# Down tiles from the 46th on turned by VectorE in squares of 32 by 32

## The reference

```python
h = modulate(rms_norm_2(x, norm_ffn[l]), sh2, sc2)        # (256, 1024)
q = (h @ w_query).reshape(B, S, PEER_HEADS, 2, HALF_KEY)   # 8 heads, two halves of 128
s1 = jnp.einsum('bshd,nd->bshn', q[..., 0, :], sub_keys1)
s2 = jnp.einsum('bshd,nd->bshn', q[..., 1, :], sub_keys2)
# top 16 of each, then the top 16 of their 256 sums: expert_idx, gates = softmax
u = jnp.take(expert_down, idx_blk, axis=0)                 # (16384, 1024) rows
act = jax.nn.gelu(jnp.einsum('bpd,bphkd->bphk', h_blk, u))
vv = jnp.take(expert_up, idx_blk, axis=0)
out = jnp.einsum('bphk,bphkd->bpd', g_blk * act, vv)
```

## Time and profile before

| | us |
|---|---|
| median of 3 runs | 1553.85 (1553.6 to 1555.4) |
| span of the profiled execution | 1550.4 |
| TensorE busy | 1510.6 (97%) |
| VectorE busy | 1013.9 (65%) |
| ScalarE busy | 663.4 (43%) |
| GpSimd busy | 425.8 (27%) |

### The profile page before, as it was taken

How to read it: one execution, slowest core, us unless ns; L and a number is a source line. 1 busy time by engine, 2 the same in 40 slices (tenths; PEclk the granted TensorE clock), 3 DMA queues, 4 the chain that set the end, 5 groups by cost and what they waited for, 6 DMA issues and landing times.

```text
span 1550.4 us, 25630 instructions
## 1 busy us (share of the span) xinstructions
PE 1510.6 (97%) x10099; PEld 1280.4 (83%) x10099; DVE 1013.9 (65%) x1829; ACT 663.4 (43%) x1009; POOL 425.8 (27%) x285
## 2 busy tenths in 40 slices
PE   8999999999999888999999999999999999999998
PEld 6777878875655575799999999999999888888887
DVE  5888787755765755678998733333334777777776
ACT  4455453633322511434434443434344444454553
POOL 0000000000011200018888888888882000000000
PEclk9999999999999999999999999999999999999999
DMA  9776664448655902446665656666663777777776
GB/s 342 268 261 226 209 239 137 162 163 258 227 207 175 407 19 67 160 147 178 137 150 137 148 139 148 140 144 143 146 142 95 239 239 242 240 238 238 239 239 231
DMA packets 166075, 297.25 MB, mean 192 GB/s; under 512 B 49539, under 2 KB 70323, under 8 KB 165957
## 3 DMA queue, kind: packets, MB, share of 16 engines
q1 hardware_dynamic: 119680, 277.08, 53.0%
q0 software_dynamic: 39296, 8.55, 7.6%
q10 hardware_dynamic: 6980, 9.99, 2.1%
HBM read 276.54 MB, written 19.03 MB: 191 GB/s over the span
## 4 chain that ended last, share of the span: by engine, by line
PE 91%; DVE 4%; issue 2%; ACT 1%; DMA 1%; SPq 0%; DVEq 0%
PE bank L553 23%; PE bank L555 22%; PE bank L557 22%; PE bank L1166 7%; PE bank L548 6%; PE bank L1097 1%; PE bank L1113 1%; PE bank L903 1%; PE bank L915 1%; PE bank L605 1%; PE bank L526 1%; PE bank L914 1%; DVE gt L1273 1%; PE bank L1157 0%; PE bank L598 0%
## 5 line engine op out<-in xcount | busy, mean ns | idle before, releaser
L2591 POOL DMA_INDIRECT c_dram<-gates,places x256 | 403.3, 1575 | 165.1 <-DVE gates L1962 87.5
L1292 DVE TENSOR_TENSOR dT_low<-bank,dT_high 128x512 fp32r<-128x512 f32 x256 | 165.0, 687 | 217.5 <-ACT dT_high L2488 150.6
L553 PE MATMUL bank<-hT_high,dT_high 128*128 128x256 f32 x1024 | 298.9, 292 | 0.1
L555 PE MATMUL bank<-hT_low,dT_high 128*128 128x256 f32 x1024 | 288.1, 281 | 0.0
L557 PE MATMUL bank<-hT_high,dT_low 128*128 128x256 f32 x1024 | 284.7, 278 | 0.0
L2500 ACT CAST up_high<-slot 128x1024 fp32r<-128x1024 f32 x128 | 134.5, 1051 | 160.1 <-DMA slot<-in_expert_up_dram 160.1
L553 PE MATMUL bank<-up_high,A_high 128*128 128x512 f32 x512 | 200.0, 391 | 1.2 <-DVE A_low L1292 1.2
L555 PE MATMUL bank<-up_low,A_high 128*128 128x512 f32 x512 | 200.7, 392 | 0.0
L557 PE MATMUL bank<-up_high,A_low 128*128 128x512 f32 x512 | 199.2, 389 | 0.0
L557 PEld LDWEIGHTS bank<-hT_high,dT_low 128*128 128x128 f32 x1024 | 193.4, 189 | 0.0
L553 PEld LDWEIGHTS bank<-hT_high,dT_high 128*128 128x128 f32 x1024 | 192.8, 188 | 0.3 <-issue 0.3
(11 more groups left out here) (449 smaller groups left out, 2370.5 us busy)
## 6 DMA issues: line engine op xcount, KB each, us to landing
slot<-in_expert_down_dram SPq DMA_DIRECT2D x128, 512.0 KB
slot<-in_expert_up_dram SPq DMA_DIRECT2D x128, 512.0 KB, 3.6
slot<-in_w_in_dram SPq DMA_DIRECT2D x41, 1024.0 KB, 5.4
P<-in_w_ada_dram SPq DMA_DIRECT2D x16, 1024.0 KB, 7.7
c_dram<-zeros SPq DMA_DIRECT2D x1, 16384.0 KB, 51.0
slot<-c_dram SPq DMA_DIRECT2D x128, 128.0 KB, 3.5
slot<-in_w_in_dram SPq DMA_DIRECT2D x6, 2048.0 KB, 8.4
slot<-in_w_out_dram SPq DMA_DIRECT2D x8, 1024.0 KB, 5.2
```

Source lines behind the costliest of these rows:

```text
L553: pe.matmul(o, lhsT=lhs_high.bitcast(F32R), rhs=rhs_high.bitcast(F32R), start=start, stop=False, skip_group_check=True)
L555: pe.matmul(o, lhsT=lhs_high.bitcast(F32R), rhs=rhs.bitcast(F32R), start=False, stop=False, skip_group_check=True)
L1292: return v.tensor_tensor(dst.bitcast(F32R), src, high, ALU.subtract)
L2591: g.indirect_dma_start(C_dram, bass.IndirectOffsetOnAxis(ap=places[:, x, k:k + 1], axis=0), gates[:, x, k:k + 1], None, compute_op=ALU.add ...
```

## The change

Tiles 0 to 44 are still turned by TensorE, tiles 45 to 127 (`BY_PE = 45`) by VectorE. The load of such a tile is split into four transfers, one for each group of 32 partitions; partition 32q+r gets, for m in 0..3, the 256 columns from 256q on of row 32m+r, in pieces of 1 KB. One `v.transpose` of 128x1024 turns all squares of 32 by 32 at once, reading every eighth column, and writes the whole turned tile, from SBUF to SBUF, into `dT_raw`, which lies where `dT_low` of that buffer lies. ScalarE copies it to `dT_high` in one instruction of 1024 columns, and VectorE subtracts in place. In VectorE's list, the turning of tile n+1 stands ahead of the subtraction of tile n and waits for the matmuls of tile n-2.

The squares give another order of inputs: block j holds the features 8p+j for partition p. So TensorE turns tiles 0 to 44 and the features `h3` from every eighth column too (`spread_block`), the query weights are loaded with rows 8p+j, and the rows 2, 3 and 5 of `modT` are loaded straight into that order (32 bytes per partition, three transfers), while only 24 rows of `mod_rows` are still turned.

```diff
--- before.py
+++ after.py
@@ -173,7 +173,7 @@
     state_ready, u_ready = sem("state_ready"), sem("u_ready")
     y_centred, y_squared, y_summed, y_rooted, bonus_v, y_done = (
         sem("y_centred"), sem("y_squared"), sem("y_summed"), sem("y_rooted"), sem("bonus_v"), sem("y_done"))
-    down_in, up_in = [sem(f"down{j}_in") for j in range(4)], [sem(f"up{j}_in") for j in range(4)]
+    down_in, up_in = [sem(f"down{j}_in") for j in range(3)], [sem(f"up{j}_in") for j in range(4)]
     h_high_ready, h_low_ready = sem("h_high_ready"), sem("h_low_ready")
     down_high, up_high, up_split, a_high_made = sem("down_high"), sem("up_high"), sem("up_split"), sem("a_high_made")
     gated, weighed, tile_done = sem("gated"), sem("weighed"), sem("tile_done")
@@ -181,6 +181,7 @@
     zeros_set, zeroed, scattered = sem("zeros_set"), sem("zeroed"), [[sem(f"scattered{t}_{h}") for h in range(2)] for t in range(TT)]
     coeff_in = [sem(f"coeff{j}_in") for j in range(4)]
     scaled_ready, bank_summed = sem("scaled_ready"), sem("bank_summed")
+    down_turned, turned_low = sem("down_turned"), sem("turned_low")
 
     cursor = [(nc.sbuf_base + 63) // 64 * 64]
 
@@ -284,6 +285,9 @@
 
     def tiles_of(x):
         return [x[:, t, k * P:(k + 1) * P] for t in range(TT) for k in range(x.shape[2] // P)]
+
+    def spread_block(x, j):
+        return x.rearrange("p (q j) -> p j q", j=KT)[:, j]
 
     def over_tokens(x, at, n):
         return x[:, at:at + n].unsqueeze(2).broadcast_to([P, n, P])
@@ -483,6 +487,16 @@
     m2_lo = carve("m2_lo", KT, S)
     C_dram = nc.dram_tensor("c_dram", [N_KEYS * N_KEYS * S, 1], F32, kind="Internal").ap()
     turn_banks = ((4, 5), (0, 1), (2, 3))
+    BY_PE = 45
+    cursor[0] = lasting_top
+    dT_raw = []
+    for j in range(3):
+        dT_raw.append(carve(f"dT_raw{j}", KT * P))
+        carve(f"dT_skip{j}", KT * P)
+
+    def down_here(eng, n):
+        eng.wait_ge(down_in[n % 3], sum(16 if m < BY_PE else 64 for m in range(n % 3, n + 1, 3)))
+
     KEPT = 64
     HALVES, PAIRS = 4, 2
     cursor[0] = gelu_at + 4 * KEPT * S
@@ -530,12 +544,13 @@
         for k in range(len(tiles) // size):
             pe_turn_bank(tag, tiles, k, size)
 
-    def pe_features(tag, tmp, base, t):
+    def pe_features(tag, tmp, base, t, spread=False):
         pe.wait_ge(normed, base + t + 1)
         for k in range(0, KT, 4):
             b = fill((tag, t, k // 4), 4 + 2 * t + k // 4)
             for n in range(4):
-                m = pe.transpose(b[:, n * P:(n + 1) * P], tmp[:, t, (k + n) * P:(k + n + 1) * P], ident)
+                x = spread_block(tmp[:, t, :], k + n) if spread else tmp[:, t, (k + n) * P:(k + n + 1) * P]
+                m = pe.transpose(b[:, n * P:(n + 1) * P], x, ident)
             m.then_inc(filled((tag, t, k // 4)), 1)
 
     def pe_sums(key, lhs, w, t, aside=None):
@@ -698,8 +713,8 @@
 
     def pe_merge():
         b = side(("modT",))
-        pe.wait_ge(mod_in, 64)
-        pe.transpose(b[:, 0:48], mod_rows[0:48, :], ident[0:48, 0:48]).then_inc(filled(("modT",)), 1)
+        pe.wait_ge(mod_in, 80)
+        pe.transpose(b[:, 0:24], mod_rows[0:24, :], ident[0:24, 0:24]).then_inc(filled(("modT",)), 1)
         for c in range(2):
             for t in range(TT):
                 if c == 0:
@@ -1043,7 +1058,7 @@
         pe_out2(1, 0, 1)
         pe_out2(0, 1, 1)
         pe_out2(1, 1, 0)
-        pe_features("h3", peer_tmp, 4, 0)
+        pe_features("h3", peer_tmp, 4, 0, spread=True)
         pe_out2(1, 1, 1)
 
     def pe_out2(c, t, half):
@@ -1066,7 +1081,7 @@
         for k in range(2):
             clear(pe, ("h3", 0, k))
         pe_query_tokens(0)
-        pe_features("h3", peer_tmp, 4, 1)
+        pe_features("h3", peer_tmp, 4, 1, spread=True)
         b = fill(("keysT",), 4)
         pe.wait_ge(peer_in, 64)
         for k in range(2):
@@ -1159,17 +1174,20 @@
         m.then_inc(filled(("score", c, t)), 1)
 
     def pe_tile_turn(n):
-        pe.wait_ge(down_in[n % 3], 16 * (n // 3 + 1))
+        down_here(pe, n)
         for k4 in range(2):
             b = fill(("turn", n, k4), turn_banks[n % 3][k4])
             for k in range(4):
-                m = pe.transpose(b[:, k * P:(k + 1) * P], down_tile[n % 3][:, (4 * k4 + k) * P:(4 * k4 + k + 1) * P], ident)
+                m = pe.transpose(b[:, k * P:(k + 1) * P], spread_block(down_tile[n % 3], 4 * k4 + k), ident)
             m.then_inc(filled(("turn", n, k4)), 1)
 
     def pe_tile_down(n):
         b = fill(("down", n), 6 + n % 2)[:, 0:S]
-        clear(pe, ("turn", n, 0))
-        clear(pe, ("turn", n, 1))
+        if n < BY_PE:
+            clear(pe, ("turn", n, 0))
+            clear(pe, ("turn", n, 1))
+        else:
+            pe.wait_ge(turned_low, n - BY_PE + 1)
         for k in range(KT):
             m = pe_three(b, dT_low[n % 3][:, k, :], dT_high[n % 3][:, k, :], hT_low[:, k, :], hT_high[:, k, :],
                          k == 0, k == KT - 1)
@@ -1198,7 +1216,7 @@
         pe_tile_turn(0)
         pe_tile_turn(1)
         for n in range(N_KEYS):
-            if n + 2 < N_KEYS:
+            if n + 2 < BY_PE:
                 pe_tile_turn(n + 2)
             pe_tile_down(n)
         for b in range(4):
@@ -1456,8 +1474,10 @@
         v_split(42)
         v_split(43)
         b = held(v, ("modT",))
-        v.tensor_copy(modT.rearrange("p a k -> p (a k)"), b[:, 0:48]).then_inc(emptied(("modT",)), 1)
+        v.tensor_copy(modT[:, 0:2, :], b[:, 0:16].rearrange("p (a k) -> p a k", a=2))
+        v.tensor_copy(modT[:, 4, :], b[:, 16:24]).then_inc(emptied(("modT",)), 1)
         clear(v, ("modT",))
+        v.wait_ge(mod_in, 80)
         for k, x in ((1, 4), (3, 5)):
             m = v.scalar_tensor_tensor(modT[:, x, :], modT[:, k, :], 1.0, modT[:, x, :], ALU.add, ALU.mult)
         m.then_inc(mod_ready, 1)
@@ -1968,6 +1988,16 @@
             v.wait_ge(down_high, 2 * n + k4 + 1)
             v_low(dT_low[n % 3][:, at, :], b, dT_high[n % 3][:, at, :]).then_inc(emptied(key), 1)
 
+    def v_square_turn(n):
+        down_here(v, n)
+        held(v, ("down", n - 3))
+        v.transpose(dT_raw[n % 3], down_tile[n % 3].rearrange("p (m c j) -> p j m c", m=4, j=KT)).then_inc(down_turned, 1)
+
+    def v_square_low(n):
+        v.wait_ge(down_high, n + BY_PE + 1)
+        v_low(dT_low[n % 3].rearrange("p k n -> p (k n)"), dT_raw[n % 3],
+              dT_high[n % 3].rearrange("p k n -> p (k n)")).then_inc(turned_low, 1)
+
     def v_choose():
         for part in range(5):
             v_top(0, 0, part)
@@ -1994,8 +2024,11 @@
             for part in range(5):
                 v_picks(c, part)
                 v_tile_turn(15 * (c - 1) + 10 + part)
-        for n in range(45, N_KEYS):
-            v_tile_turn(n)
+        v_square_turn(BY_PE)
+        for n in range(BY_PE, N_KEYS):
+            if n + 1 < N_KEYS:
+                v_square_turn(n + 1)
+            v_square_low(n)
 
     def v_gate(p):
         clear(v, ("down", p))
@@ -2098,10 +2131,10 @@
     def a_mod_loads():
         for j in range(2):
             a.wait_ge(mod_out[j], 16 * EARLY // 4)
-        for n, (at, g) in enumerate(((0, 0), (16, 3))):
-            a_load(mod_rows[at:at + 16, :], mod_dram[0, g * D:(g + 2) * D].rearrange("(r p) -> r p", p=P), mod_in)
-        a_load(mod_rows[32:40, :], I["norm_mix_2"][0].rearrange("(r p) -> r p", p=P), mod_in)
-        a_load(mod_rows[40:48, :], I["norm_ffn_2"][0].rearrange("(r p) -> r p", p=P), mod_in)
+        a_load(mod_rows[0:16, :], mod_dram[0, 0:2 * D].rearrange("(r p) -> r p", p=P), mod_in)
+        a_load(mod_rows[16:24, :], I["norm_mix_2"][0].rearrange("(r p) -> r p", p=P), mod_in)
+        for x, row in ((2, mod_dram[0, 3 * D:4 * D]), (3, mod_dram[0, 4 * D:5 * D]), (5, I["norm_ffn_2"][0])):
+            a_load(modT[:, x, :], row.rearrange("(p j) -> p j", j=KT), mod_in)
 
     def a_sb_score(i):
         for j in range(2):
@@ -2482,6 +2515,10 @@
     def a_tile_turn(n):
         if n > 2:
             held(a, ("down", n - 3))
+        if n >= BY_PE:
+            a.wait_ge(down_turned, n - BY_PE + 1)
+            a.copy(dT_high[n % 3].rearrange("p k n -> p (k n)").bitcast(F32R), dT_raw[n % 3]).then_inc(down_high, 1)
+            return
         for k4 in range(2):
             key, at = ("turn", n, k4), slice(4 * k4, 4 * k4 + 4)
             b = held(a, key).rearrange("p (k n) -> p k n", k=4)
@@ -2679,12 +2716,23 @@
     def s_tail_half(m):
         i = chunk_at[TAIL[m // 2]]
         _, w, c0, n = chunks[i]
-        sp.dma_start(tail_view(m), w[tail_rows(m % 2), c0:c0 + n].rearrange("(k p) n -> p k n", p=P)).then_inc(half_in[m % 4], 16)
+        at = slice(m % 2 * KT // 2, (m % 2 + 1) * KT // 2)
+        rows = (w[:, c0:c0 + n].rearrange("(p j) n -> p j n", j=KT)[:, at, :] if m > 3 else
+                w[tail_rows(m % 2), c0:c0 + n].rearrange("(k p) n -> p k n", p=P))
+        sp.dma_start(tail_view(m), rows).then_inc(half_in[m % 4], 16)
 
     def s_down(n):
-        if n > 2:
+        if n - 3 >= BY_PE:
```

(10 more changed lines are left out.)

## The result

| | before | after |
|---|---|---|
| median of the runs beside each other (5 and 5) | 1555.4 us (1553.6 to 1556.8) | 1575.15 us (1573.7 to 1585.7) |
| ratio | | 1.0142, 95% interval 1.0114 to 1.0169 |
| span of the profiled execution | 1550.4 | 1584.4 |

The change costs 20 us, 1.4%. The forecast was +70 us at 1624. The profiled execution of after is its longest one, 1585.7 us where the other four took 1574 to 1576; the last experiment takes that apart.

A forecast was written before the change was run, and what follows sets the result against it. TensorE's queue was taken as the bound, the scatters' queue as second chain; held scatters lengthen it by 80.7, so the up stage starts 68.7 later: 1553.85 + 68.7 + 1.7 (clock) = 1624 us, range 1555 to 1645.

The forecast's parts named there:

- the second chain: GpSimd's queue of 256 scatters, which must end before the coefficients load and the up stage starts; ends 20 us ahead.
- T = 1.22: Duration in us of VectorE's turning of one 128x1024 down tile, taken from nearest rows; range kept 0.75 to 2.3.
- the beat: Time from one down tile to the next where VectorE turns; claimed 2.83 us, kept by TensorE with nothing to spare.
- the lock of one scatter per tile: Beside tiles 45 to 127 each subtraction holds a scatter: 83 at 2.83 in place of 1.858, +80.7 us.
- rival D: Down stage much slower through the turning: 1739 us at 4.9, or 1667 if a 2.3 turning holds GpSimd; chance 0.11.
- The rule for the beat: In the down stage, half of what VectorE's turning takes above 1.24 us is added to TensorE's 2.83 per tile.
- The threshold of 2.96: In the down stage, one scatter passes per tile as long as the time per tile stays under 2.96 us.
- rival B: Down tiles 2.96 to 3.5 us apart, so scatters fall out of step: 1561 to 1565, mixtures to 1600; chance 0.17.
- The cap of 12 us on a gain: Before the up stage, the scatters' end would limit any gain to 12 of the 72 us taken off TensorE.
- rival C: In the down stage the subtraction holds no scatter and the kernel gets faster, 1543.5 us; chance 0.10.
- The clock, 1.7 us: TensorE, idle some 140 us, starts the up stage at the lower clock: +1.7 us, bounds 0 and 2.
- Parts priced at nothing: Stepped weight loads (0 to 0.87 a tile, hidden), features before the first scatter (0 to 1 us), modT loads, query loads.

The follow-up runs named there:

- the last experiment: The changed kernel measured once more, nothing altered: 1577.6 us, 1.0138 of the kernel before; its profiled span is 1575.9 us.
- e1_half_scatters: The changed kernel with half of the scatters left out (8 of 16 gates of each head): 1527.1 us, 0.9822 of the kernel before.
- e2_psum_91: The changed kernel with turnings written to PSUM and TensorE turning tiles 0 to 90, VectorE only 91 to 127: 1542.5 us, 0.9918 of the kernel before.
- e3_half_dense: The changed kernel with each VectorE turning in two instructions of 512 columns, first dense, second every eighth column: 1572.2 us, 1.0114 of the kernel before.
- e1_turn_dense: The changed kernel with VectorE's turning reading its tile densely instead of every eighth column: 1623.6 us, 1.0442 of the kernel before.
- e1_raw_in_psum: The changed kernel with VectorE's turned tile written to PSUM in two instructions of 128x512, not to SBUF: 1542.55 us, 0.9920 of the kernel before.

## Why the prediction was wrong

- **What bounds, and the second chain: right.** TensorE's queue and the scatters' queue are the two chains, and the change shortens the first and lengthens the second. The scatters' end decides the time in every kernel above but e1_half_scatters, the four in which TensorE turns all tiles, and e2_psum_91.
- **A scatter that starts beside an instruction with two SBUF inputs ends 1.43 us after it: right**, on nine rows, and for this shape too. What nine rows could not show is that one that starts up to 0.05 us ahead can be held as well; the single row at 759.60, 0.03 ahead and free, was one of two outcomes.
- **T = 1.22: the step that failed.** It measured 2.21, so VectorE became the full engine and the beat passed 2.96: 3.32 in place of 2.83, and the lock of one scatter per tile was lost. The nearest rows that I took T from read densely, and dense it is 1.25. The upper bound of 2.3 held it. The rule on cachelines stood in the prediction, but beside rival D and not in the term that it bears on. It gives no size, but with it T belonged above the dense rows.
- **The rule for the beat: right.** "Half of what T has above 1.24 is added": with T = 2.21 that gives 2.83 + 0.48 = 3.31 (measured 3.32), with e3_half_dense's 0.71 + 1.16 less an overlap of 0.07 it gives 3.11 (3.12), and with 1.25 it gives 2.83 (2.84). At 2.21 VectorE is busy 271 of 276 us, so its own work alone gives nearly the same beat and the change itself hardly tests the rule; e3_half_dense and e1_turn_dense do, where VectorE had idle time (18 and 39 of 220 us).
- **The threshold of 2.96: consistent, not located.** A beat of 2.84 locked (1623.6), one of 3.12 did not (1572.2); nothing was measured between them. With the beat at 3.32 rival B is what happened. A sum that stands 0.13 us from a threshold worth 50 us should not have given 0.62 to one side, least of all with T in no row.
- **Rival B's time, 1561 to 1565: 10 us short of the median.** At this T it counted five scatters in three tiles, 2.01 each, and the same first scatter. Measured were 2.10 and 2.16 (6 to 10 scatters fewer in the stage's 277 us, at 1.858 each 11 to 19 us of queue) and a first scatter 4.6 to 6.6 us later. Its 7.9 us from the queue's end to the first up matmul were 6.4.
- **The cap of 12 us on a gain: right.** e1_raw_in_psum measured -12 us; rival C's sum was 1543.5 and the kernel took 1542.55. Some of this closeness is luck: in its profiled execution the first scatter came 5.0 us later than before, and the queue's end lay 6.3 and not 7.9 ahead of the up stage.
- **The clock, 1.7 us: near.** The up stage took 2.0 us longer than before in the profiled execution of after.
- **Parts priced at nothing.** modT's loads and the query rows: nothing. Stepped weight loads: 0.042 us a tile, near the lower of the bounds 0 and 0.87. The first scatter was priced at 0 to 1, with a move of over 2 us named as a sign of being wrong, and that sign came: it starts at 694.4 to 696.4 in the three kernels with one part of the order, and at 696.4 to 699.4 in after's family, where before had 692.9 in its one profile. An estimate from these few starts: some 3 us are spread between executions, and some 3 more come with the order of inputs as a whole. Which part of it was not settled.
- **Rival D's worse half, a turning that holds GpSimd: excluded.** The 83 scatters of the stage that began beside a turning and over 0.06 us ahead of the subtraction took 1.55 to 1.57. The 22 held ones that also began beside a turning, just ahead of a subtraction, ended 1.43 after the subtraction.

## What to carry to other kernels

When work moves off the full engine, look first at the longest queue beside it, and at which memory the operands of the new instructions lie in, since that can hold this queue: here the same turning with its result in PSUM makes the kernel 0.8% faster, and in SBUF 1.4% slower. A hold between two periodic streams can lock them in whole numbers (one scatter per tile, three in two, five in three), so the cost jumps with the beat, and less work can cost more: 1623.6 us with the shorter turning, 1572.2 with the longer. Work out the thresholds and give chances by the distance to them. The duration of an instruction is taken from a row with the same access pattern, not just the same count of elements.

## What the runs showed of the hardware

- A VectorE transpose in squares of 32 by 32, f32, 128x1024: 1.25 us dense, 2.21 with steps of 32 bytes. For 128x512: 0.71 dense, 1.06 with 16 bytes (into PSUM), 1.15 to 1.16 with 32.
- It reads one input and held none of 83 scatters; a subtraction with both inputs in SBUF holds one that starts while it runs until 1.43 us after its end, and often one that starts up to 0.05 us ahead (22 held, 6 free). The Trainium skill (SBUF — State Buffer, Who interferes with whom) infers that descriptor generation is not held by a tensor_tensor; 79 scatters in 220 us in e1_turn_dense say otherwise for these indirect transfers. Whether it is their descriptors that wait, or the reading of `places` from SBUF, no run tells.
- TensorE transposes that load every eighth column as weights cost 5 ns more each, 277 in place of 272, though the weight load itself takes 193 in place of 140 (medians).
